# The split input operand of a three-pass float32 kernel, moved 64 bytes within its SBUF row

## The reference

```python
h  = x + pos_embed_2d(...)                 # 256 latent tokens
hc = ctx                                   # 256 context tokens
h  = h  + 0.5 * ml[:, 2] * swiglu(modulate(rmsnorm(h, g0),  ml[:, 0], ml[:, 1]), ffn_w_in[0], ffn_w_out[0])
hc = hc + 0.5 * mc[:, 2] * swiglu(modulate(rmsnorm(hc, g0), mc[:, 0], mc[:, 1]), ffn_w_in[0], ffn_w_out[0])
pl = modulate(rmsnorm(h, g1),  ml[:, 3], ml[:, 4]) @ w_in     # head projections and pooling columns
pc = modulate(rmsnorm(hc, g1), mc[:, 3], mc[:, 4]) @ w_in
...                                        # gated DeltaNet scans over 8 heads, pooling mixer
h  = h + ml[:, 5] * mixer_out(pl, ...)     # w_out, latent tokens only
h  = h + 0.5 * ml[:, 8] * swiglu(modulate(rmsnorm(h, g2), ml[:, 6], ml[:, 7]), ffn_w_in[1], ffn_w_out[1])
return rmsnorm(h, final_g)
```

## The kernel before

| moving, stationary | columns | before | after |
|---|---|---|---|
| `xh`/`xl`, `wh`/`wl` (FFN 1, heads) | 512, 256 | 0 | 64 |
| `xh`/`xl`, `eh`/`el` and `wbah`/`wbal` (heads) | 512, 256 | 0 | 64 |
| `wh`/`wl`, `xh`/`xl` (pooling columns) | 512 | 0 | 448 |
| `hth`/`htl`, `wh`/`wl` (FFN 1 down, last group) | 512 | 0 | 0 |
| `yh`/`yl`, `wh`/`wl` (output projection) | 256 | 64 | 64 |
| `x2h`/`x2l`, `wh`/`wl` (FFN 2 up) | 256 | 64 | 64 |
| `hth2`/`htl2`, `wh`/`wl` (FFN 2 down) | 256 | 192 | 192 |
| `ada_t`, `cpad` (adaLN) | 256 | 0 | 64 |
| `wp`, `u` (pooling mixer, plain float32; in the trace `u,wp`) | 256 | 128 | 128 |

## Time and profile before

### The profile page before, as it was taken

One profiled execution on the slowest core, in us unless ns is written; L12 is line 12 of the kernel. 1 busy time (PEld: TensorE's weight loads), 2 busy tenths in 40 slices (PEclk: granted clock), 3 DMA queues, 4 the chain that ended last, 5 costly groups with the idle time before them and its releaser, 6 DMA issues. The chain is left out here.

```text
span 2885.8 us, 47636 instructions
## 1 busy us (share of the span) xinstructions
PE 2832.5 (98%) x17840; PEld 2487.4 (86%) x17840; DVE 1647.3 (57%) x2212; ACT 968.2 (34%) x1443; POOL 212.8 (7%) x373
## 2 busy tenths in 40 slices
PE   6999999999999999999999999999999999999998
PEld 4788888888888888888888888878999999999998
DVE  5567667667677652222226666756665555555555
ACT  3222222222222222112214555544454343433444
POOL 0000000000000000000001113464210000000001
PEclk8999999999999999999999999999999999999999
DMA  9867677677888855655563666686455555655564
GB/s 375 290 210 218 196 223 218 199 220 247 317 308 298 316 180 199 196 176 180 191 195 91 171 194 189 201 251 196 151 172 185 187 182 182 189 186 184 183 190 144
DMA packets 410321, 604.41 MB, mean 209 GB/s; under 512 B 52961, under 2 KB 303841, under 8 KB 401521
## 3 DMA queue, kind: packets, MB, share of 16 engines
q1 hardware_dynamic: 361824, 419.52, 46.3%
q10 hardware_dynamic: 48400, 183.63, 19.1%
HBM read 560.02 MB, written 43.02 MB: 209 GB/s over the span
## 5 line engine op out<-in xcount | busy, mean ns | idle before, releaser
L1945 DVE TENSOR_TENSOR wl<-raw,wh 128x1024 fp32r<-128x1024 f32 x638 | 781.1, 1231 | 816.2 <-ACT wh L1470 813.1
L1470 ACT CAST wh<-raw 128x1024 fp32r<-128x1024 f32 x638 | 664.7, 1047 | 1461.4 <-PE ps L763 1442.4
L762 PE MATMUL ps<-xl,wh 128*128 128x512 f32 (+1 forms) x2560 | 970.0, 379 | 0.0
L761 PE MATMUL ps<-xh,wh 128*128 128x512 f32 (+1 forms) x1904 | 724.5, 381 | 0.8 <-DVE wl L1945 0.7
L763 PE MATMUL ps<-xh,wl 128*128 128x512 f32 (+1 forms) x1904 | 718.3, 377 | 0.0
L762 PEld LDWEIGHTS ps<-xl,wh 128*128 128x128 f32 x2560 | 483.2, 189 | 90.2
L761 PEld LDWEIGHTS ps<-xh,wh 128*128 128x128 f32 x1904 | 359.9, 189 | 75.8 <-issue 8.9
L763 PEld LDWEIGHTS ps<-xh,wl 128*128 128x128 f32 x1904 | 359.5, 189 | 66.7
L761 PE MATMUL ps<-x2h,wh 128*128 128x256 f32 x1408 | 395.6, 281 | 1.7 <-DVE x2l L2015 1.7
L763 PE MATMUL ps<-x2h,wl 128*128 128x256 f32 x1408 | 394.0, 280 | 0.0
L762 PE MATMUL ps<-x2l,wh 128*128 128x256 f32 x1408 | 393.9, 280 | 0.0
(11 more groups left out here) (276 smaller groups left out, 2649.2 us busy)
## 6 DMA issues: line engine op xcount, KB each, us to landing
raw<-in_ffn_w_in SPq DMA_DIRECT2D x704, 256.0 KB, 3.5
raw<-in_ffn_w_out SPq DMA_DIRECT2D x176, 512.0 KB, 4.3
abuf<-in_w_ada ACTq DMA_DIRECT2D x64, 1024.0 KB, 7.0
abuf<-in_w_ada ACTq DMA_DIRECT2D x96, 512.0 KB, 4.0
xl<-d_h ACTq DMA_DIRECT2D x80, 512.0 KB, 3.4
ada_t<-in_ada SPq DMA_DIRECT2D x64, 512.0 KB, 9.0
raw<-in_w_in SPq DMA_DIRECT2D x128, 256.0 KB, 3.5
raw<-in_w_out SPq DMA_DIRECT2D x32, 512.0 KB, 5.1
```

The lines of the kernel that those rows point to most:

```text
L761: mm(out, ah, bh, start=first, stop=False, skip_group_check=reopened)
L762: mm(out, ah, bl, start=False, stop=False, skip_group_check=reopened)
L1470: nc.scalar.copy(wh[:, t % HL, :], raw[:, t % RAW, :]).then_inc(hi_done, 1)
L1945: tt(tl, raw[:, t % RAW, :], th.bitcast(F32), ALU.subtract).then_inc(lo_done, 1)
```

## The change

Three placements change, and no instruction is added, removed or moved; every engine's list is the same.

```diff
@@ -245,9 +245,9 @@
         with ExitStack() as both:
+            sb("apart3", [P, KT], stack=both)
             xh = sb("xh", [P, KT, NTOK], F32R, stack=both)
             xl = sb("xl", [P, KT, NTOK], F32R, stack=both)
-            b1 = sb("b1", [P, KT], stack=both)
         sb("apart2", [P, KT])
@@ -287,13 +287,13 @@
             arow = sb("arow", [P, 2, ADA_W], stack=st)
+            b1 = sb("b1", [P, KT], stack=st)
             with ExitStack() as first:
                 ada_t = sb("ada_t", [P, ADA_RING, KT // ADA_Q, ADA_W], stack=first)
             with ExitStack() as later:
-                sb("apart", [P, KT], stack=later)
                 hth2 = sb("hth2", [P, GROUP_FF, SEQ], F32R, stack=later)
                 htl2 = sb("htl2", [P, GROUP_FF, SEQ], F32R, stack=later)
-            sb("apart1", [P, 6 * KT], stack=st)
+            sb("apart1", [P, 5 * KT], stack=st)
             hth = sb("hth", [P, GROUP_FF, NTOK], F32R, stack=st)
```

## The result

The changed kernel takes 2896.23 us (median of 20 runs, 2886.25 to 2903.02); the kernel before, run beside it, 2885.32 us (20 runs, 2876.60 to 2890.47). The ratio is 1.0042, with a 95% interval of 1.0033 to 1.0052: slower by 0.4%, 12 us by the ratio. The forecast was 2868.2, and the range of 2830 to 2892 doesn't hold the time.

A forecast was written before the change was run, and what follows sets the result against it. TensorE's matmul count and start-to-start interval were taken as the bound. Savings of 9.1 + 4.4 + 3.5 + 0.4 us, 17.5 with unrounded terms, off the median 2885.67 gave 2868.2 us; 8-in-10 range 2830 to 2892.

The forecast's parts named there:

- What bounds the kernel: FFN 1 and head projections: TensorE alone sets the end, by its number of matmuls and the interval between their starts.
- The surplus of 32 cycles at offset 0 depends on the placement: FFN 1: 226.7 ns a matmul against 213.3 for 512 columns; moving and weight streams start at the same address modulo 512 bytes.
- nothing happens: Rival: the two SBUF readers don't affect each other, 2.2 ns comes from something else, time stays 2885.7 us; chance 0.17.
- 120.0 becomes 117.8 ns at 64, 256 columns: Closing tiles of FFN 1 down: their 256-column matmuls should come every 117.8 instead of 120.0 ns.
- carry the saving of 2.24 ns over to 512 columns: 512-column matmuls: the saving seen on 256 columns taken as fixed per matmul, 226.7 becomes 224.4 ns; no row shows it.
- FFN 1 up was forecast at -9.1 us: FFN 1 up, `xh` and `xl` as moving operand: 4080 matmuls by 2.24 ns, 9.1 us saved, all on the path.
- FFN 1 down was forecast at -4.4: FFN 1 down, blocks fetched into `xl`: 1968 matmuls by 2.24 ns, 4.4 us saved; the 192 with `hth` give nothing.
- Heads and pooling columns: Head projections: 1584 matmuls by 2.24 ns, 3.5 us saved; 192 pooling columns, operands turned, priced the same, 0.4 us.
- The rest at nothing: Shifted `ada_t` (covered by transfer waits), `b1` elsewhere, transfers into `xl`, VectorE and ScalarE writes: no change in time.
- The rival that the surplus goes wholly: 512-column matmuls fall to 215 ns, about 2807 us, or a mix at 2848 to 2856; chance 0.17 for 2807 to 2859.
- The slower rival: 512-column streams met in mid-stream lose more; 7 ns up on FFN 1's 5952 costs 42 us, 2927; chance 0.19.

The follow-up runs named there:

- slots64: Changed kernel with `xh`, `xl` back at offset 0; FFN 1 down's slots shifted 64 bytes (first pass), 0 to 48 (second); ratio 1.0041 to the kernel before.
- columns: `xh`, `xl` at 0; FFN 1 down's fetched blocks cut to 128, 256, 384, 512 moving columns by slot, passes at offsets 0 and 64; work left out, 2764.13 us.

## Why the prediction was wrong, point by point

- **What bounds the kernel**: right. TensorE has no idle time in FFN 1 after either, and the 15.2 us by which the stretch up to the heads is longer are in its intervals.
- **The surplus of 32 cycles at offset 0 depends on the placement**: right, slots64 shows it by a shifted view alone. The rival "nothing happens" falls. The prediction had tied it to the rule of the Trainium skill, "SBUF — State Buffer", section "Who interferes with whom"; as far as that rule would make the placement of TensorE's two operands free, it doesn't hold here: the same matmuls have 226.7 and 233.3 ns at two placements.
- **120.0 becomes 117.8 ns at 64, 256 columns**: right, in the closing tiles of FFN 1 down and, mixed, in the heads.
- **"I take it as a cost per matmul and its weight load that doesn't grow with the columns, and carry the saving of 2.24 ns over to 512 columns"**: this is the step that failed. The equal surplus of 256 and 512 columns holds at offset 0 only. At 64 it is 26.7, 32 and 37 cycles for 256, 384 and 512 columns (label columns), so 512 columns went to 228.9 ns. FFN 1 up was forecast at -9.1 us and came at +11.1 with the adaLN stage before it: from 248 us on 3540 matmuls x 2.2 ns = 7.8 us, between 127 and 248 us some 520 at 233.3 in place of 226.7 ns, 3.4 us. Of these 3.4 us, 2.3 come from the second level, which no row of before could show. FFN 1 down was forecast at -4.4 and came at +4.1.
- **Heads and pooling columns**: forecast -3.5 and -0.4. The projections came at -2.4, the right direction. It was partly luck, since the reason given, a fixed saving at each width, doesn't hold: in the mixed stream of the heads the 512-column matmuls sat at 231.7 ns before, not at 226.7, and came down by 1.4 ns. The pooling columns got slower by 4.8 ns each, 0.9 us, where 0.4 us less was forecast.
- **The rest at nothing**: right. The other engines' busy times didn't move, and the long stretch of FFN 1 up behind the adaLN products starts at 121.8 us before and 121.9 after.
- **The rival that the surplus goes wholly** falls: none of the sixteen multiples of 16 bytes brought a 512-column float32r stream below 226.7 ns. The prediction's estimate of 215.7 ns, from the figure of the Trainium skill, "TensorE: Matmul & The Clock Gate", section "Wait — 56ns, not 53.3ns?", is not seen on it at any offset.
- **The slower rival** was the right one in direction, with a wrong size. It had 7 ns a matmul and 2927 us; measured are 2.2. Its argument, that a longer stream loses more, fits the run columns; that it loses it by meeting the weight load isn't shown, since a load of 0.11 us in place of 0.19 made the interval longer. Its evidence in the trace, 396 ns of a matmul's duration in the heads, spoke of a stream of mixed widths and not of the offset.

What stays open: whether the two streams contend for something and for what, why the period is 256 bytes, and what decides between the two levels after an interruption. The forecast also rested on one profile of the kernel before, with `hth2` at 117.8 ns at offset 192; that 192 can give 113.4 didn't show there.

## What to carry to other kernels

The distance between the moving and the stationary operand of a matmul, modulo 256 bytes here, is a tuning parameter of its own, and its best value depends on the number of columns: a value measured on one shape is not to be carried to another. It can be scanned cheaply, by shifted views of one stage within one profiled kernel, and read from the starts of matmuls; the busy time doesn't show it. It has to be measured against what a stage varies by when nothing in it changes, here up to 4 us. Where single runs of a kernel fall into groups, look whether a stage has two intervals for the same instructions before believing a difference of half a per cent.

## What the runs showed of the hardware that I had not expected

- The interval of float32r matmuls depends on that distance with a period of 256 bytes: 512 columns from 226.7 ns (0 and 240) over 228.9 (64) to 234.7 (208), 256 columns from 113.4 (192) to 120.0 (0).
- A stream can hold one of two intervals with nothing different in the program: 113.4 or 117.8 ns at 192 with 256 columns, 229 or 233 ns at 64 with 512. In the kernel before the runs fall into two groups some 10 us apart, and with `hth2` moved to 64 the lower group is gone (twelve runs, none below 2880).
- A shorter weight load doesn't shorten the interval at offset 0: 231.7 ns with 32 columns of weights against 226.8 with 128.
- The version with the lowest median, x0_all192, keeps all 512-column operands at 0 and puts all 256-column ones of the output projection and FFN 2 at 192: 0.9941 of the time before. Six of its ten runs lie some 26 us below the median of the kernel before, as FFN 2 at the short interval would have it, and four are level with it.
